# Weight chunks of one decoder trunk loaded in pairs of 1 MB instead of singly

## What is computed

```python
for l in range(2):
    hn = rmsnorm(x, norm_mix[l])
    y = even_mixer(hn, ...) if l % 2 == 0 else odd_mixer(hn, ...)     # input projection, mix, output projection
    x = x + y
    x = x + conv_ffn(rmsnorm(x, norm_ffn[l]), w_up[l], conv_w[l], conv_b[l], w_down[l])

def conv_ffn(h, w_up, conv_w, conv_b, w_down):
    u = causal_dwconv(h @ w_up, conv_w, conv_b)                       # 2048 -> 2 x 5632
    gate, val = jnp.split(u, 2, axis=-1)
    return (jax.nn.gelu(gate) * val) @ w_down                         # 5632 -> 2048
```

## Time and profile before

| | |
|---|---|
| median of three runs | 2207.36 us |
| the profiled execution | 2208.97 us |
| its span | 2207.2 us |
| TensorE matmuls busy | 2200.5 us (100%), weight loads 1839.5 us |
| VectorE busy | 1507.4 us (68%) |
| ScalarE busy | 1158.5 us (52%) |
| granted TensorE clock | 1.00 throughout |
| SP's DMA queue | 479.67 MB, 69.8% of 16 engines |

### The profile page before, as it was taken

How to read it: one execution, slowest core, us unless ns; L and a number is a source line. 1 busy time by engine, 2 the same in 40 slices (tenths; PEclk the granted TensorE clock), 3 DMA queues, 4 the chain that set the end, 5 groups by cost and what they waited for, 6 DMA issues and landing times.

```text
span 2207.2 us, 29263 instructions
## 1 busy us (share of the span) xinstructions
PE 2200.5 (100%) x10238; PEld 1839.5 (83%) x10238; DVE 1507.4 (68%) x1907; ACT 1158.5 (52%) x1447; POOL 7.7 (0%) x17
## 2 busy tenths in 40 slices
PE   9999999999999999999999999999999999999999
PEld 8888888888888888888888888888888888888887
DVE  7886766777777777655566566576777677766454
ACT  6654445555655564444455555555556556554443
POOL 0000000000000000000000000000000000000000
PEclk9999999999999999999999999999999999999999
DMA  8555567777787777766676675577777878777665
GB/s 275 181 179 172 181 201 229 213 245 237 238 248 230 244 241 251 220 202 208 204 237 192 217 230 162 191 219 233 228 249 232 249 228 248 233 248 240 211 217 163
DMA packets 261459, 486.99 MB, mean 221 GB/s; under 512 B 18069, under 2 KB 50341, under 8 KB 261248
## 3 DMA queue, kind: packets, MB, share of 16 engines
q1 hardware_dynamic: 259488, 479.67, 69.8%
q0 software_dynamic: 1456, 5.65, 0.7%
q10 hardware_dynamic: 432, 0.56, 0.1%
HBM read 450.65 MB, written 35.15 MB: 220 GB/s over the span
## 4 chain that ended last, share of the span: by engine, by line
PE 97%; DMA 1%; DVE 1%; issue 0%; ACT 0%; SPq 0%; ACTq 0%; DVEq 0%
PE ps L853 18%; PE ps L855 18%; PE ps L854 18%; PE ps L809 10%; PE ps L835 8%; PE ps L837 8%; PE ps L836 8%; PE ps L813 5%; DMA h<-turn_line 1%; PE ps L892 0%; PE ps L947 0%; PE ps L874 0%; PE ps L893 0%; PE ps L955 0%; PE ps L886 0%
## 5 line engine op out<-in xcount | busy, mean ns | idle before, releaser
L1101 DVE TENSOR_TENSOR w_lo<-raw,w_hi 128x1024 fp32r<-128x1024 f32 x783 | 947.7, 1222 | 560.5 <-ACT w_hi L473 534.0
L473 ACT ACTIVATE w_hi<-raw 128x1024 fp32r<-128x1024 f32 x783 | 810.9, 1055 | 634.2 <-PE ps L837 249.9
L853 PE MATMUL ps<-w_hi,xs 128*128 128x512 f32 x1856 | 724.2, 390 | 0.1
L854 PE MATMUL ps<-w_lo,xs 128*128 128x512 f32 x1856 | 722.2, 389 | 0.0
L855 PE MATMUL ps<-w_hi,xs 128*128 128x512 f32 x1856 | 722.2, 389 | 0.0
L853 PEld LDWEIGHTS ps<-w_hi,xs 128*128 128x128 f32 x1856 | 348.4, 188 | 73.7 <-DVE w_lo L1101 1.9
L855 PEld LDWEIGHTS ps<-w_hi,xs 128*128 128x128 f32 x1856 | 348.3, 188 | 72.6
L854 PEld LDWEIGHTS ps<-w_lo,xs 128*128 128x128 f32 x1856 | 348.4, 188 | 71.7
L835 PE MATMUL ps<-w_hi,act 128*128 128x512 f32 x808 | 314.8, 390 | 0.9 <-DVE w_lo L1101 0.9
L837 PE MATMUL ps<-w_hi,act 128*128 128x512 f32 x808 | 314.4, 389 | 0.0
L836 PE MATMUL ps<-w_lo,act 128*128 128x512 f32 x808 | 314.3, 389 | 0.0
(11 more groups left out here) (203 smaller groups left out, 1159.0 us busy)
## 6 DMA issues: line engine op xcount, KB each, us to landing
raw<-w_up SPq DMA_DIRECT2D x352, 512.0 KB, 4.6
raw<-w_in SPq DMA_DIRECT2D x191, 512.0 KB, 4.0
raw<-w_down SPq DMA_DIRECT2D x176, 512.0 KB, 4.7
raw<-w_out SPq DMA_DIRECT2D x64, 512.0 KB, 4.8
turn_line<-cross SPq DMA_DIRECT2D x252, 128.0 KB, 2.3
h<-turn_line SPq DMA_DIRECT2D x63, 512.0 KB, 5.9
bias<-bias_line POOLq DMA_DIRECT2D x1, 2048.0 KB, 10.4
x_res<-x_t SPq DMA_DIRECT2D x3, 512.0 KB, 7.2
```

What stands on the lines that cost most here:

```text
L473: act_f(w_hi[:, s, :, :], raw[:, s, :, :], ACT.Copy).then_inc(hi_ready, 1)
L853: mm(out, x_hi, w_hi[:, s, u, :], start=first and u == 0, stop=False)
L854: mm(out, x_hi, w_lo[:, s, u, :], start=False, stop=False)
L1101: tt(w_lo[:, s, :, :], raw[:, s, :, :], w_hi[:, s, :, :].bitcast(F32), ALU.subtract).then_inc(lo_ready, 1)
```

## The change

`load` issues nothing for odd chunks. For an even chunk it waits until the split of the chunk three before it is done (`s + 2` instead of `s + 1`, so both slots of the pair are free) and loads 512 rows, two chunks, into two neighbouring slots with one DMA of 1 MB. There is one semaphore `landed` for each pair of slots. Chunk 0 is still loaded in two tiles, and chunk 1 by a DMA of its own with the semaphore `second_landed`. All else stays in its place in SP's list. What stood between the loads of an even chunk and its odd neighbour now stands behind both.

```diff
-    landed = [sem(f"landed{s}") for s in range(RING)]
+    landed = [sem(f"landed{k}") for k in range(RING // 2)]
+    second_landed = sem("second_landed")
+    raw_pairs = raw[:, :, :, :].rearrange("p (k u) t n -> p k (u t) n", u=2)
...
             s = c % RING
             turn = q + c // RING
+            if s % 2:
+                return
             if not (isinstance(turn, int) and turn == 0):
 
-                sp.wait_ge(lo_ready, RING * (turn - 1) + s + 1)
-            src = w[bass.ds(rows * (CT * P), CT * P), cols].rearrange("(t p) n -> p t n", p=P)
-            sp.dma_start(raw[:, s, :, :], src).then_inc(landed[s], 16)
+                sp.wait_ge(lo_ready, RING * (turn - 1) + s + 2)
+            src = w[bass.ds(rows * (CT * P), 2 * CT * P), cols].rearrange("(u t p) n -> p (u t) n", u=2, p=P)
+            sp.dma_start(raw_pairs[:, s // 2, :, :], src).then_inc(landed[s // 2], 16)
...
-                    load(w_in[l], ph.q_in + 2 * b, c, slice(col, col + NB), c)
+                    if (l, b, c) == (0, 0, 1):
+                        src = w_in[0][CT * P:2 * CT * P, col:col + NB].rearrange("(t p) n -> p t n", p=P)
+                        sp.dma_start(raw[:, 1, :, :], src).then_inc(second_landed, 16)
+                    else:
+                        load(w_in[l], ph.q_in + 2 * b, c, slice(col, col + NB), c)
...
             s, turn = c % RING, q + c // RING
-            eng.wait_ge(landed[s], 16 * (turn + 1))
+            if isinstance(turn, int) and turn == 0 and s == 1:
+                eng.wait_ge(second_landed, 16)
+            else:
+                eng.wait_ge(landed[s // 2], 16 * (turn + 1))
```

## The result

The changed kernel took 2361.31 us (median of 6 runs, 2358.23 to 2363.07), the kernel before 2207.85 us in the same comparison. The ratio is 1.0688 with a 95% interval of 1.0678 to 1.0699. The forecast was 2373 us, in a range of 2265 to 2465.

A forecast was written before the change was run, and what follows sets the result against it. The prediction took TensorE as the bound, with the up projection's round-trip loop equal within 0.6%. Its terms, 154 + 7 + 5 = 166 us on the profiled 2208.97, gave 2375 us, or 2373 as a median; range 2265 to 2465.

The forecast's parts named there:

- The bound and its cover: Up-projection round-trip loop takes 21.89 us per half against TensorE's 21.76, so a longer loop is paid nearly in full.
- (b): On SP in the up projection, the put queues behind the load of chunks 6 and 7: 2.1 us later by order alone.
- (a): Half as many loads on SP (0.37 us per issue): SP only waits here, so nothing on the path.
- (c): Up projection: the put's data lie behind 1 MB, so the fetch is issued 8.5 us after the transposes instead of 4.0.
- (d): Up projection: the fetch, again behind 1 MB, takes 5.6 us and lands 14.1 us after the transposes.
- (e): Each up-stage interval becomes 25.6 us against TensorE's 21.76: 3.84 us more, 42 times, 154 us after deductions.
- (f): Entries of the up stages: one delay of 3.7 us per layer from the output projection's last round trip, 7 us (0 to 12).
- (g): Weights: even chunks land about 4 us later, mostly hidden by TensorE's cover outside the up stages; 5 us in all (0 to 20).
- The loop itself: Up projection: transposes, put, landing, fetch, landing, L1256, taps, next transposes; an interval is the fetch's landing plus 11.5 us.
- The other signs: VectorE waits 120 to 160 us for fetched tiles, TensorE some 160 us behind `w_lo`, nearly all in up stages; clock 1.00.
- Relief: Rival, 2%: half as many DMAs free the queue, the fetch lands sooner, the loop drops under TensorE's 21.76 us: 2202 us.

## Why the prediction was right, point by point

**The bound and its cover.** Right. The loop of the round trip was within 0.6% of TensorE's own 8 chunks, its 11.5 us behind the landing held in every half, and pairing is free where no round trip stands near (ratio 1.0006, with two DMAs per pair).

**(b) The place of the put.** Right: transposes end at 1693.52, put at 1695.51, 2.0 us later (2.1 forecast). Term (a), that SP's issues are not on the path, holds only behind the put: the second issue ahead of it in the kernel with two DMAs per pair moved it by another 0.6 us.

**(c) The data ahead of the put.** Right in kind, a little too small. From the load to the fetch I took 7.2 us; the two halves shown have 1678.33 - 1671.22 = 7.1 and 1703.00 - 1695.03 = 8.0. Over the loop halves the fetch was issued 9.0 us after the transposes, where T+8.5 was forecast. I had said that I take the two lower readings, but 6.5 is the lowest alone. Half of the data took 1.1 us per interval off.

All four DMAs of this put landed behind the 1 MB (its load at 1671.22 took 5.8 us, to 1677.0, and the first of the put, issued at 1671.70, took 5.5, to 1677.2). By the rule of strongly ordered increments (the Trainium skill, "DMA: Bandwidth & Descriptors", Queues, rings and completion order) it must be so, and this trace agrees. In all 44 puts of the two stages the landing of the first DMA reads between 0.2 us ahead of that of its 1 MB and 0.7 behind (both rounded to 0.1): with it or later, never clearly before. A queue that simply finishes in order would look the same. The issues of the first half:

```profile
raw<-w_up SPq DMA_DIRECT2D x1, 1024.0 KB, 5.8
...
turn_line<-cross SPq DMA_DIRECT2D x4, 128.0 KB, 5.4
...
h<-turn_line SPq DMA_DIRECT2D x1, 512.0 KB, 3.7
```

**(d) The fetch.** Too large, and wrong in kind. I took 5.6 us for every half; the mean is 4.6. Where VectorE has only splits behind the transposes, the load ahead is issued early (1674.26) and the fetch takes 3.7, as the last row above shows. In the other halves, with more work between the splits, that load comes late (1699.58) and the fetch takes 5.5. The landings are 1682.0 and 1708.5. That is 12.3 us after the transposes that ended at about 1669.7, and 15.0 us after those that ended at 1693.5, 13.7 on average, where 14.1 was forecast. Over all loop halves it is 12.6 and 14.6 in turn, 13.5 on average. The prediction had only one half of the kernel before to go by, the shorter kind: 10.0 us there, 10.6 in its neighbours.

**(e) The interval.** 25.0 us instead of 25.6: the size of this term was off. The stages grew by 128 us instead of 154. That the miss is no larger is partly luck: the fetch was issued 0.5 us later than forecast (c) and landed 1.0 us sooner after its issue (d), and the two errors nearly halve each other. The distance of 11.5 us held: the fetch landed at 1708.5, the transposes ended at 1720.05.

**(f), (g) Entries and the rest.** 12 us forecast, 22.6 measured, and all of it where (f) had 12 as its upper bound. The kernel with single loads beside the round trips has none of it, so it is the round trips at the edges of the up stages, and (g) is nothing, not 5 us. Put to put, 11.1 us lie ahead of the first put of the first stage (422.04 against 410.94), 11.5 between the two stages and none behind the last put. The place of (f) was right, its mechanism too narrow: it counted one delay of 3.7 us per layer for the last round trip of the output projection, but at that put the changed kernel is already 7.3 us behind (373.05 against 365.71), and the first up blocks add the rest. One of the prediction's signs misleads here. It said that large waits of ScalarE for `raw` in the down stages would put the cost on (g). They came, 154.6 us where there had been 17.9, and TensorE did not notice them:

```profile
ACT w_hi L484 <- DMA raw<-w_down: 154.6, 54, 6.2
```

The two errors, 26 us down and 11 us up, account for most of the distance from 2373 to 2361.

**The loop itself** was incomplete. The landings of chunks 6, 7 and 0 are gates of it too. In the changed kernel they close before the fetch, so the forecast did not suffer. But in the longer halves they do so by a hair: behind the split of chunk 0, ScalarE's first tap at 1710.01 waited only 0.27 us for L1267. Leaving these gates out put the kernels with an earlier fetch 19 to 105 us outside their expected bands, once with the wrong sign (the fetch moved in the kernel before).

**The other signs.** VectorE's waits for the fetched tile came to 116.5 us over both stages (120 to 160 forecast) and TensorE's behind `w_lo` to 133.0 (160 forecast). The clock did not stay at 1.00 as forecast (see the last section).

**Relief.** The queue's share fell while it moved the same data:

```profile
q1 hardware_dynamic: 253232, 479.64, 61.6%
```

Before it was 259488 packets, 479.67 MB, 69.8% of a shorter span. That is 0.698 x 2207 = 1541 against 0.616 x 2358 = 1453 us of a mean engine. The Trainium skill's rule that larger transfers use the bandwidth better ("Perfetto Trace Analysis", DMA Optimizations) would explain it, but the runs do not bear that out: the kernel with the same order and two DMAs of 512 KB per pair has 61.7% of 2369 us, 1462. At most 9 of the 88 us go with the size, the rest with the order. The fixed 2.0 us per DMA that the prediction took from the Trainium skill ("DMA: Bandwidth & Descriptors", Anatomy of one DMA) is stated there for DMAs that GpSimd issues, while these loads are issued by SP, and no run here measures it. In any case no stage waited for bandwidth, only for the order of landings.

## What to carry to other kernels

Before loads are merged, list what stands between them in the issuing queue: each item moves by one load in order and by its transfer in the queue, and a round trip through DRAM that closes a loop pays both every time around. Compare the period of such a loop with the bound engine's before trusting a profile in which that engine is 100% busy; here 21.9 against 21.8 us meant that a single `if` moved by one chunk cost 47 us. And a loop has a gate for each landing that stands in front of one of its steps on any engine, so a shorter round trip alone may give nothing.

## What was not expected of the hardware

TensorE's granted clock was 1.00 throughout before and 0.992 on average after: it fell to its lower level of 1.2 GHz in eleven short stretches at the entries and in the loops of the up stages, where TensorE had just waited (busy 8.21 of 10 us in the one shown). In the kernel whose TensorE waited most, with the fetch alone moved, it was 0.973. The sum of the waits does not decide it: with put and fetch ahead the weight loads waited 127.1 us for `w_lo`, nearly the 133.0 of the changed kernel, at a clock of 0.998. A window of the changed kernel (busy time of each engine, granted clock, DMA share, GB/s):

```profile
680.00:690.00 10.00, 8.21 (x30) 6.32 (x29) 4.72 (x6) 7.65 (x10) 0.00 (x0) 0.83 0.48 182
```

The half with that stretch took 696.71 - 670.76 = 25.95 us from put to put, and one without (1695.51 to 1722.05) 26.54. Nine of the 18 longer halves of the loops have such a stretch. They took 26.1 us on average, and the nine without 26.2. So in this loop the slower clock falls into time in which TensorE would have waited, and no cost shows from put to put. That need not hold at the entries, where two of the stretches lie. Of the six runs of the changed kernel, the three with a mean clock of 0.992 took 2358.23 to 2361.18 us and the three with 0.990 or 0.991 took 2361.45 to 2363.07. Whether the clock costs these 2 to 3 us or longer waits cost both was not tried by a run of its own.
